# U and V expert rows gathered in turn, diagonal weights formed ahead of the routing, attention slots between quads of weighted rows

## What is computed

```
s_top, i_top = lax.top_k(s, PEER_TOPK)
cand = s_top[:, :, 0, :, None] + s_top[:, :, 1, None, :]
sc, ci = lax.top_k(cand.reshape(n, PEER_HEADS, PEER_TOPK * PEER_TOPK), PEER_TOPK)
...
e = i1 * PEER_N_KEYS + i2
gate = jax.nn.softmax(sc, axis=-1)
act = jax.nn.gelu(jnp.einsum('nd,nhkd->nhk', h, expert_u[e]), approximate=False)
return jnp.einsum('nhk,nhkd->nd', gate * act, expert_v[e])
```

## Time and profile before

| | |
|---|---|
| median of 3 runs | 3973.64 us |
| lowest and highest | 3964.76 and 3981.46 us |
| the profiled execution's own time | 3969.55 us |
| its span, first to last instruction | 3967.8 us |
| TensorE busy | 2900.9 us (73%) |
| VectorE busy | 2817.0 us (71%) |
| GpSimd busy | 2265.1 us (57%) |
| ScalarE busy | 906.5 us (23%) |
| moved by transfers | 1388.40 MB, 1216.48 of them by GpSimd's queue |

### The profile page before, as it was taken

One profiled execution on the slowest core, in us unless ns is written; L12 is line 12 of the kernel. 1 busy time (PEld: TensorE's weight loads), 2 busy tenths in 40 slices (PEclk: granted clock), 3 DMA queues, 4 the chain that ended last, 5 costly groups with the idle time before them and its releaser, 6 DMA issues.

```text
span 3967.8 us, 41980 instructions
## 1 busy us (share of the span) xinstructions
PE 2900.9 (73%) x12200; PEld 1426.3 (36%) x12200; DVE 2817.0 (71%) x6758; ACT 906.5 (23%) x1933; POOL 2265.1 (57%) x2286
## 2 busy tenths in 40 slices
PE   7979986987678788846877788884757775455545
PEld 5656763665234334412332244441223231011101
DVE  6677874335866787878767767777886678877773
ACT  1344212432111244411111144441111111000000
POOL 1101212012666677777766667777776666767775
PEclk9999997988789878878888977877887887777777
DMA  7567997235899999999999999999999999999998
GB/s 254 204 252 261 416 380 270 82 105 214 335 411 410 396 343 350 358 382 371 410 410 410 403 341 360 388 358 385 405 396 410 410 408 379 382 405 398 408 406 326
DMA packets 420421, 1388.40 MB, mean 350 GB/s; under 512 B 46055, under 2 KB 122535, under 8 KB 407903
## 3 DMA queue, kind: packets, MB, share of 16 engines
q0 software_dynamic: 306432, 1216.48, 78.2%
q1 hardware_dynamic: 87534, 140.06, 10.1%
q10 hardware_dynamic: 26224, 29.15, 2.1%
HBM read 1332.98 MB, written 56.86 MB: 350 GB/s over the span
## 4 chain that ended last, share of the span: by engine, by line
DMA 23%; POOL 21%; PE 13%; issue 12%; DVE 8%; PEld 3%; DVEq 1%; ACT 1%; PEldq 0%; ACTq 0%; POOLq 0%; SPq 0%
POOL st_rows L1474 21%; DMA st_rows<-in_peer_v,st_expert_v 19%; PE st_ps_y L1897 5%; DMA st_rows<-in_peer_u,st_expert 3%; DVE st_rows L2202 3%; PE st_ps_q L1813 2%; PE st_ps_m L1823 2%; PE st_ps_m L1760 1%; PE st_ps_t L1794 1%; PE st_ps_m L1829 1%; PEld st_ps_t L1794 0%; PEld st_ps_y L1949 0%; PE st_ps_y L1912 0%; DMA st_in_sb<-scr_o_sb 0%; PE st_ps_q L1852 0%
## 5 line engine op out<-in xcount | busy, mean ns | idle before, releaser
L1897 PE MATMUL st_ps_y<-st_rows,st_diag 128*32 128x512 f32 x4096 | 1104.7, 653 | 636.1 <-DMA st_rows<-in_peer_v,st_expert_v 610.9
L1474 POOL DMA_INDIRECT st_rows<-in_peer_u,st_expert x1024 | 1061.3, 1036 | 451.8 <-issue 288.2
L1474 POOL DMA_INDIRECT st_rows<-in_peer_v,st_expert_v x1024 | 1050.8, 1026 | 468.9 <-issue 281.7
L2202 DVE CUSTOM_DVE_ANT_0 st_rows<-st_rows,st_ps_m 128x1024 f32<-128x1024 f32 x624 | 745.1, 1220 | 323.1 <-DMA st_rows<-in_peer_u,st_expert 302.4
L1897 PEld LDWEIGHTS st_ps_y<-st_rows,st_diag 128*32 128x32 f32 x4096 | 204.7, 115 | 1497.1 <-DMA st_rows<-in_peer_v,st_expert_v 837.7
L2202 DVE CUSTOM_DVE_ANT_0 st_rows<-st_rows,st_h 128x1024 f32<-128x1024 f32 x400 | 475.6, 1221 | 72.4 <-DMA st_rows<-in_peer_u,st_expert 66.2
L612 PE MATMUL pd_ps<-pd_w,pd_xnT 128*128 128x256 f32 x1152 | 266.1, 388 | 26.9 <-issue 20.6
L1852 PE MATMUL st_ps_q<-st_shared 128*128 128x128 f32 (+3 forms) x1024 | 242.0, 397 | 6.5 <-DMA st_shared<-in_w_pq_heads 3.0
L612 PEld LDWEIGHTS pd_ps<-pd_w,pd_xnT 128*128 128x128 f32 x1152 | 219.6, 194 | 73.6 <-issue 36.6
L439 POOL DMA_INDIRECT pd_kv<-in_cache_v,pd_rows x32 | 49.3, 1539 | 330.6 <-DVE pd_z L875 214.4
L1852 PEld LDWEIGHTS st_ps_q<-st_shared 128*128 128x128 f32 x1024 | 181.3, 200 | 59.8 <-issue 11.6
(11 more groups left out here) (334 smaller groups left out, 3975.8 us busy)
## 6 DMA issues: line engine op xcount, KB each, us to landing
st_shared<-in_w_pq_heads SPq DMA_DIRECT2D x32, 1024.0 KB, 8.1
st_rows<-in_peer_u,st_expert POOLq DMA_INDIRECT x1024, 11.2
st_rows<-in_peer_v,st_expert_v POOLq DMA_INDIRECT x1024, 11.2
pd_w<-in_w_in SPq DMA_DIRECT2D x14, 1024.0 KB, 10.0
scr_proj<-pd_stage ACTq DMA_DIRECT2D x8, 1152.0 KB, 18.0
st_rows<-scr_factors SPq DMA_DIRECT2D x20, 416.0 KB
scr_score<-st_sc_out ACTq DMA_DIRECT2D x64, 130.0 KB
st_sc<-scr_score SPq DMA_DIRECT2D x64, 130.0 KB, 6.2
```

The costliest lines, as they stand in the source:

```text
L1474: pool.indirect_dma_start(rows[n % R][:, :], None, src, bass.IndirectOffsetOnAxis(ap=idx, axis=0)).then_inc(row_loaded[n % R], 16)
L1897: ins = nc.tensor.matmul(ps_y[j * QUAD:(j + 1) * QUAD, c * 512:(c + 1) * 512], diag[k % 2][:, QS * j + q, :], rows[n % R][:, c * 512:(c + ...
L2202: nc.vector.tensor_tensor_reduce(out=rows[n % R][:, :], in0=rows[n % R][:, :], in1=hb, scale=1.0, scalar=0.0, op0=ALU.mult, op1=ALU.add, a ...
```

## The change

The rings, the loads and every operation's shape stay. What changes is the order in which rows are gathered and consumed, and where three pieces stand. In GpSimd's order the U rows of step k and the V rows of step k-1 alternate one by one (in step 0 there are only U rows, behind step 63 only V rows). VectorE forms the weights right behind the dots, then the best keys of step k+2, then `value_inputs(k)`, and only then routes; `read_sums` stands ahead of the dots instead of behind the tenth. TensorE takes the values quad by quad: behind each quad come the attention slots that VectorE has behind the same four dots (`slots_behind`), the score head stands behind quad 1, and `spread_both(k)` ahead of a second score head.

```diff
--- before.py
+++ after.py
@@ -1061,8 +1061,9 @@
     stores_upto = lambda g: sum(len(MIX_GROUPS[x]) for x in range(g + 1))
     route_no = lambda k: k if k <= SAMPLE_ROUTE_STEP + 2 else k + 1
     SAMPLE_ROUTE_NO = SAMPLE_ROUTE_STEP + 3
-    row_u = lambda k, s: (32 * k - K if k > 0 else 0) + (2 * H if k > SAMPLE_AFTER else 0) + s
-    row_v = lambda k, s: (32 * k + 2 * K if k + 1 < STEPS else 32 * k + K) + (2 * H if k >= SAMPLE_AFTER else 0) + s
+    row_u = lambda k, s: (2 * K * k - K + 2 * s if k > 0 else s) + (2 * H if k > SAMPLE_AFTER else 0)
+    row_v = lambda k, s: 2 * K * k + K + (2 * s + 1 if k + 1 < STEPS else s) + (2 * H if k >= SAMPLE_AFTER else 0)
+    slots_behind = lambda k, s: ATTEND.get(k, ())[s * len(ATTEND.get(k, ())) // (K - 2):(s + 1) * len(ATTEND.get(k, ())) // (K - 2)]
     row_su = lambda s: 32 * SAMPLE_AFTER + K + s
     row_sv = lambda s: 32 * SAMPLE_AFTER + K + H + s
     read_at = {H * b + H + 1: b for b in range(FB - 1) if H * (b + 1) != SAMPLE_AFTER}
@@ -1474,26 +1475,28 @@
                 pool.indirect_dma_start(rows[n % R][:, :], None, src,
                                         bass.IndirectOffsetOnAxis(ap=idx, axis=0)).then_inc(row_loaded[n % R], 16)
 
-            def gather_values(k):
-
-                pool.wait_ge(ev_ready, k + 1)
-                for s in range(K):
-                    c = QS * (s % QS) + s // QS
-                    gather(row_v(k, s), v_rows, expert_v[k % 4][:, c:c + 1])
+            def gather_value(k, s):
+
+                c = QS * (s % QS) + s // QS
+                gather(row_v(k, s), v_rows, expert_v[k % 4][:, c:c + 1])
 
             for k in range(STEPS):
                 pool.wait_ge(e_ready, k + 1)
+                if k > 0:
+                    pool.wait_ge(ev_ready, k)
                 for s in range(K):
                     gather(row_u(k, s), u_rows, expert[k % 4][:, s:s + 1])
-                if k > 0:
-                    gather_values(k - 1)
+                    if k > 0:
+                        gather_value(k - 1, s)
                 if k == SAMPLE_AFTER:
                     pool.wait_ge(te_ready, 1)
                     for s in range(H):
                         gather(row_su(s), u_rows, te[:, s:s + 1])
                     for s in range(H):
                         gather(row_sv(s), v_rows, te[:, s:s + 1])
-            gather_values(STEPS - 1)
+            pool.wait_ge(ev_ready, STEPS)
+            for s in range(K):
+                gather_value(STEPS - 1, s)
 
         @block.scalar
         def _(act):
@@ -1882,24 +1885,25 @@
                 ins.then_inc(spread_ready, 1)
                 spreads["n"] = n + 1
 
-            def values(k):
+            def values(k, q):
 
                 b, hd = k // H, k % H
-                if hd == 0 and k > 0:
-                    pe.wait_ge(y_read, k // H + (k >= SAMPLE_AFTER))
-                pe.wait_ge(diag_ready, k + 1)
-                for q in range(QS):
-                    for c in range(2):
-                        for j in range(QS):
-                            n = row_v(k, QS * q + j)
-                            if c == 0:
-                                pe.wait_ge(row_loaded[n % R], 16 * (n // R + 1))
-                            ins = nc.tensor.matmul(ps_y[j * QUAD:(j + 1) * QUAD, c * 512:(c + 1) * 512], diag[k % 2][:, QS * j + q, :],
-                                                   rows[n % R][:, c * 512:(c + 1) * 512],
-                                                   start=(hd == 0 and q == 0), stop=(hd == H - 1 and q == QS - 1), skip_group_check=True)
-                            if c == 1:
-                                ins.then_inc(row_used[n % R], 1)
-                pe.drain().then_inc(v_done, 1)
+                if q == 0:
+                    if hd == 0 and k > 0:
+                        pe.wait_ge(y_read, k // H + (k >= SAMPLE_AFTER))
+                    pe.wait_ge(diag_ready, k + 1)
+                for c in range(2):
+                    for j in range(QS):
+                        n = row_v(k, QS * q + j)
+                        if c == 0:
+                            pe.wait_ge(row_loaded[n % R], 16 * (n // R + 1))
+                        ins = nc.tensor.matmul(ps_y[j * QUAD:(j + 1) * QUAD, c * 512:(c + 1) * 512], diag[k % 2][:, QS * j + q, :],
+                                               rows[n % R][:, c * 512:(c + 1) * 512],
+                                               start=(hd == 0 and q == 0), stop=(hd == H - 1 and q == QS - 1), skip_group_check=True)
+                        if c == 1:
+                            ins.then_inc(row_used[n % R], 1)
+                if q == QS - 1:
+                    pe.drain().then_inc(v_done, 1)
 
             def sample_values():
 
@@ -2004,19 +2008,22 @@
                     turn(TURN[k])
                 if k in MIX:
                     mix(MIX[k])
-                for g, t in ATTEND.get(k, ()):
-                    attend(g, t)
                 heads = SCORE.get(k, ())
-                for g, hd in heads[:1]:
-                    score_head(g, hd)
-                if k > 0:
-                    values(k - 1)
+                for q in range(QS):
+                    if k > 0:
+                        values(k - 1, q)
+                    for s in range(QS * q, QS * q + QS):
+                        for g, t in slots_behind(k, s):
+                            attend(g, t)
+                    for g, hd in heads[:1] if q == 1 else ():
+                        score_head(g, hd)
+                spread_both(k)
                 for g, hd in heads[1:]:
                     score_head(g, hd)
-                spread_both(k)
                 if k == SAMPLE_AFTER:
                     sample_values()
-            values(STEPS - 1)
+            for q in range(QS):
+                values(STEPS - 1, q)
 
         @block.vector
         def _(dve):
@@ -2209,15 +2216,11 @@
                     dve.wait_ge(h_loaded[b % 2], 16 * (b // 2 + 1))
                 if FREE[k]:
                     dve.wait_ge(h_copied, copies_upto(k))
-                slots = ATTEND.get(k, ())
+                if k in read_at:
+                    read_sums(k // H - 1 + (k > SAMPLE_AFTER), read_at[k])
                 for s in range(K):
                     dot(row_u(k, s), ps_m[:, :] if FREE[k] else h[b % 2][:, :], act_in[k % 2][:, s:s + 1])
-                    if s == 9:
-                        if k > 0:
-                            value_inputs(k - 1)
-                        if k in read_at:
-                            read_sums(k // H - 1 + (k > SAMPLE_AFTER), read_at[k])
-                    for g, t in slots[s * len(slots) // (K - 2):(s + 1) * len(slots) // (K - 2)]:
+                    for g, t in slots_behind(k, s):
                         attend(g, t)
                 dve.drain().then_inc(dots_ready, 1)
 
@@ -2351,8 +2354,10 @@
             route(1)
             for k in range(STEPS):
                 dots(k)
+                weights(k)
                 if k + 2 < STEPS:
                     best_keys(k + 2, 0)
+                value_inputs(k)
                 if k == 0:
                     query_norms(0, tuple(range(2, H)))
                 b, hd = divmod(k + 2, H)
@@ -2360,7 +2365,6 @@
                     query_norms(GROUP_OF[b][0], (hd,))
                 if k + 2 < STEPS:
                     route(k + 2)
-                weights(k)
                 if k == SAMPLE_ROUTE_STEP:
                     route_sample()
                 if k == SAMPLE_ROUTE_STEP + 1:
@@ -2387,7 +2391,6 @@
                                             t_weight[:, :].unsqueeze(2).broadcast_to([P, H, NS]), ALU.mult)
                     dve.drain().then_inc(t_diag_ready, 1)
                     second_norm(SAMPLE_AFTER // H - 1)
-            value_inputs(STEPS - 1)
             read_sums(FB, FB - 1)
             second_norm(FB - 1)
```

## The result

The changed kernel takes 4925.4 us (4912.6 to 4939.3, four runs), the kernel before took 3977.6 in the same session. The ratio is 1.242, 95% interval 1.237 to 1.246. The forecast was 4680 with a range up to 4880: the sign and the mechanism held, the size did not (+948 us where +711 was forecast), and the time lies outside the range.

The account below looks back on a forecast made before the run. Transfers were taken to bound plain and two-head steps, but not attention steps. Terms 285 + 144 + 13 + 204 + 72 - 7 = +711 us on the profiled 3969.6 gave 4681, stated as 4680, range 4360 to 4880.

Parts of the forecast that it names:

- The central mechanism: Place 13 of a step's rows waits for VectorE's first dot; routing no longer overlaps transfers; plain step 44.1 us.
- The landing time: Plain step: a gather lands in 6.2 us, so the dots end 30.1 us after the first dot starts.
- the gap: VectorE's own work from a step's last dot to the next first dot: 14.0 us in a plain step.
- Mix +285: Eight steps projecting a mixed block: first V row waits for the projection; 83.3 us each, 666 in all, +285 us.
- Score +144: Sixteen steps with one score head: the head between quads delays the last U row; 876 against 732.1 us, +144.
- Attention +204: Seventeen steps with attention slots: quads between slots add 11.4 us of TensorE time, VectorE's gap 0.5; +204 us.
- rival (b): Attention steps: quads waiting for their last row hold up the slots behind; +240 us, total 4920; chance 0.08.
- Two heads +13: Four steps with two score heads: 50 us each with one query norm, 204 against 190.7 us, +13.
- the other 18 +72: Remaining 18 steps: 16 plain bodies with norms, scales, the sample's route and dots; 869 against 797 us, +72.
- (a): Heads and slots overlap with rows in flight; only mix steps and bare stalls remain: +363 us, 4340; chance 0.14.
- (c): Attention steps are lifted to the transfer bound: 109 us go, 3865; chance 0.05.
- (d): The reordering does not bind, since the ring drains the same 32 rows: within 0.5%, 3974; chance 0.03.

Follow-up runs that it names:

- experiments 2 and 10: 2: changed kernel with 15 ring tiles instead of 13, 4637.5 us; 10: changed kernel, eight V rows behind last U row, 5080.7 us; spread also moved, 4405.4 us.
- experiment 4: Three more VectorE operations behind each routing: kernel before 4447.15 us against 4447.23 beside it on another chip; changed kernel 5055.7 us.
- Experiment 5: Changed kernel with the inputs of the values read behind the routing instead of between best keys and route: 4816.8 us.
- Experiment 7: Changed kernel with each quad of values behind its group of attention slots instead of ahead, in the 17 attention steps: 4829.0 us.

## Why the prediction was wrong in size

- **The central mechanism** (place 13 waits for the first dot; routing stands in series) held: GpSimd's stop, the next dot without a wait, and experiments 2 and 10 show it; experiment 4 (0 against 130 us) agrees.
- **The landing time** was taken as 6.2 us and measured 6.9; D came out 31.0 against 30.1.
- **The step that failed is the gap**, in the terms for the tail and the spread: "a quad's tail takes 1.9 and the spread 1.2 ... the two are level", and "TensorE's clock is no part of the argument". The 1.9 was right for the kernel before, where 58 of the 59 tails with the spread right behind took it (the spread, which the earlier trace rows do not show, took 1.05 in 61 of 65). In it V rows came one every 1.28 us. With one every 2.5 us the granted clock is lower (0.68 over steps 58 to 62, 0.75 before; 0.50 around the tail of step 60), and of the 48 such tails of the changed kernel 42 took more than 3 us; of its 65 spreads 28 took 1.89 and 31 still 1.05.
- **What that costs.** In step 60 the spread ends 7.2 us after the last U row has landed, not 4.4: 1.7 for the tail, 0.7 for the spread and 0.4 between the two that the sum left out. With 1.90 and 1.05 in the same rows the wait of 3.42 us would be 0.9, by my estimate. The gap of a plain step with routing became 16.3 instead of 14.0 (steps 58 to 61 take 47.3 on average, D 31.0). Times the 46 steps without attention this is 106 us. VectorE waits 137 us for the spread in them, where the forecast had nothing. Experiment 5, which takes the wait away, gained 109, and its gaps are the forecast's: 13.6 in plain steps with routing (14.0), 17.5 in score steps (17.8), 27.2 in mix steps (27.4). The Trainium skill has the rule that would have warned ("TensorE: Matmul & The Clock Gate", section "What's actually happening"): the throttled state is the default, and activity releases it. The rows agree: 3.62 us after waits for rows, 1.90 when idle matmuls filled them.
- **Mix +285** measured 305: D 55.8 against 55.9, the projection's chain step by step; all of the difference is in the gap, 30.0 against 27.4.
- **Score +144** measured 216: D was 38.5 and 35.5 in the forecast, 40.8 and 35.8 measured, which is 21 of the 72 us; the other 51 are the gap, 21.0 on average where the forecast adds up to 17.8.
- **Attention +204** measured 259. The forecast took the quads' busy time (11.4 us), and gave waits for rows, rival (b), a chance of 0.08. Experiment 7 gives back 91 us in these steps by another place for the same matmuls. The right reading of the earlier trace rows was not that TensorE is full, but that slots and quads form one chain: whatever waits in it is added. Neither the forecast nor the rival alone is what happened: the waits grew by 98 us (75.7 to 174) and not by 240. That rival (b)'s total, 4920, is 5 us from the result is luck: it puts 444 us into the attention steps, which lost 259, and nothing into the gaps. What the rest of the attention term is made of stays open. The misses of gap, attention and score steps all have the same sign, and the range was made from each alone.
- **Two heads +13** measured 29, **the other 18 +72** measured 136: gap and landing once more, as far as the five plain steps among them show. The tail's -7 measured -2.5.
- Rivals (a), (c) and (d) are out: no step class became faster, and the smallest loss is 3.4 us a step.

## What to carry to other kernels

When two consumers share one ring in strict turn, each serial stretch of either (routing, a projection, a head) stops both after as many rows as the ring holds; find the longest stretch in which one consumer takes nothing, and ask what the other can still be given. Work that is hidden in one order can cost its full length in another: the same 2.4 us of VectorE cost 2.1 a step in the changed kernel. A duration read where rows come densely need not hold where they are spaced out (1.90 and 3.62 us for the same ten matmuls here), and a wait that was hidden behind a slower one (the spread behind the V rows) must be priced anew when the order is loosened as well as when it is tightened.

## What the chip showed that I had not expected

- One and the same group of ten value matmuls takes 1.90 or 3.62 us, and the eight of the spread 1.05 or 1.89, near the factor of two between the levels 2.4 and 1.2 GHz, at a granted clock of 1.00 and 0.50. Ahead of the slow ones TensorE had taken one V row every 2.5 us, with pauses of 0.6 to 1.5 between them.
- Reading two tables in turn cost nothing (3969.2 against 3970.0).
- A gather's landing varied from 4.2 to 9.0 us in the plain steps of the changed kernel, where GpSimd stands still before each step's first dot; in the plain steps before it was 10.6 to 13.2.
- With eight V rows behind the last U row, steps 20 to 27 ran at 402 GB/s with a score head still in each.
